# Matmul columns taken in pieces by turns from two halves, and operands set apart, in an fp32r transformer kernel

## What is computed

```python
h = h + 0.5 * swiglu(rms_norm(h, ffn1_norm), ffn1_wi, ffn1_wo)   # halves a1, b1, c1
h = h + mixer(rms_norm(h, mix_norm))                             # gla, dsa, mla
h = h + 0.5 * swiglu(rms_norm(h, ffn2_norm), ffn2_wi, ffn2_wo)   # halves a2, b2, c2
def swiglu(x, wi, wo):
    gate, up = jnp.split(x @ wi, 2, axis=-1)                     # 1024 -> 2 * 2816
    return (jax.nn.silu(gate) * up) @ wo                         # 2816 -> 1024
```

## Time and profile before

| | |
|---|---|
| median of 2 runs | 1460.05 us (1460.01 to 1460.09) |
| the profiled execution | 1459.98 us |
| its span, first to last instruction | 1458.1 us |
| TensorE busy | 1451.5 us, granted clock 1.0 of 2.4 GHz |
| weight loads busy | 1250.3 us |
| VectorE busy | 1002.2 us (69%) |
| ScalarE busy | 777.7 us (53%) |
| DMA | 183 GB/s mean |

### The profile page before, as it was taken

How to read it: one execution, slowest core, us unless ns; L and a number is a source line. 1 busy time by engine, 2 the same in 40 slices (tenths; PEclk the granted TensorE clock), 3 DMA queues, 4 the chain that set the end, 5 groups by cost and what they waited for, 6 DMA issues and landing times.

```text
span 1458.1 us, 18627 instructions
## 1 busy us (share of the span) xinstructions
PE 1451.5 (100%) x7822; PEld 1250.3 (86%) x7822; DVE 1002.2 (69%) x1216; ACT 777.7 (53%) x971; POOL 87.1 (6%) x113
## 2 busy tenths in 40 slices
PE   9999999999999999999999999999999999999999
PEld 7888888888888888888888888888888888888887
DVE  6876466777755877459877764787646987687753
ACT  6654355655534555345665544565436876465542
POOL 0000003000000000006100000000000800000000
PEclk9999999999999999999999999999999999999999
DMA  9855563556556555545465556465556543566552
GB/s 328 277 176 185 159 204 116 167 180 201 178 184 200 190 181 195 185 141 172 149 200 188 185 177 206 154 223 182 188 173 217 188 145 118 173 196 201 179 188 72
DMA packets 205620, 266.82 MB, mean 183 GB/s; under 512 B 6944, under 2 KB 148880, under 8 KB 205280
## 3 DMA queue, kind: packets, MB, share of 16 engines
q1 hardware_dynamic: 204320, 261.23, 54.7%
q0 software_dynamic: 1072, 4.35, 0.8%
q10 hardware_dynamic: 144, 0.05, 0.0%
HBM read 264.56 MB, written 1.05 MB: 182 GB/s over the span
## 4 chain that ended last, share of the span: by engine, by line
PE 93%; DVE 3%; ACT 1%; DMA 1%; issue 0%; SPq 0%; DVEq 0%; ACTq 0%
PE ps L631 31%; PE ps L638 17%; PE ps L563 14%; PE ps L565 13%; PE ps L564 13%; PE ps L616 1%; DMA raw<-in_ffn_wi 1%; DVE wlo L1656 1%; PE ps L741 1%; PE ps L836 1%; PE ps L774 1%; DVE d_i L2049 0%; ACT whi L1217 0%; DVE d_m L2045 0%; DVE d_i L2073 0%
## 5 line engine op out<-in xcount | busy, mean ns | idle before, releaser
L1656 DVE TENSOR_TENSOR wlo<-raw,whi 128x2048 fp32r<-128x2048 f32 (+5 forms) x275 | 567.3, 2068 | 259.1 <-ACT whi L1217 258.9
L1217 ACT CAST whi<-raw 128x2048 fp32r<-128x2048 f32 (+5 forms) x275 | 474.0, 1729 | 223.0 <-PE ps L565 218.5
L631 PE MATMUL ps<-xt,whi 128*128 128x512 f32 x2112 | 501.7, 391 | 0.8 <-DVE xt L2249 0.7
L631 PEld LDWEIGHTS ps<-xt,whi 128*128 128x128 f32 x2112 | 389.3, 188 | 78.0 <-DVE xt L2249 1.5
L638 PEld LDWEIGHTS ps<-xt,wlo 128*128 128x128 f32 x2112 | 267.1, 191 | 8.2
L638 PE MATMUL ps<-xt,wlo 128*128 128x256 f32 x2112 | 269.6, 283 | 0.0
L563 PE MATMUL ps<-whi,xt 128*128 128x512 f32 (+4 forms) x304 | 112.7, 371 | 0.0
L565 PE MATMUL ps<-whi,xt 128*128 128x512 f32 (+4 forms) x304 | 109.7, 361 | 0.0
L564 PE MATMUL ps<-wlo,xt 128*128 128x512 f32 (+4 forms) x304 | 109.5, 360 | 0.0
L563 PEld LDWEIGHTS ps<-whi,xt 128*128 128x128 f32 x304 | 57.3, 189 | 9.2 <-issue 1.0
L565 PEld LDWEIGHTS ps<-whi,xt 128*128 128x128 f32 x304 | 57.2, 188 | 8.5
(11 more groups left out here) (422 smaller groups left out, 1884.3 us busy)
## 6 DMA issues: line engine op xcount, KB each, us to landing
raw<-in_ffn_wi SPq DMA_DIRECT2D x85, 1024.0 KB, 5.0
raw<-in_ffn_wo SPq DMA_DIRECT2D x40, 1024.0 KB, 4.9
raw<-in_ffn_w_gate SPq DMA_DIRECT2D x22, 1024.0 KB, 5.1
raw<-in_ffn_w_up SPq DMA_DIRECT2D x22, 1024.0 KB, 5.1
raw<-in_ffn_w_down SPq DMA_DIRECT2D x20, 1024.0 KB, 4.9
raw<-in_w_in SPq DMA_DIRECT2D x14, 1024.0 KB, 5.1
raw<-in_even_w_in SPq DMA_DIRECT2D x6, 1024.0 KB, 5.2
raw<-in_ffn_wo SPq DMA_DIRECT2D x8, 512.0 KB, 3.8
```

What stands on the lines that cost most here:

```text
L631: return e.matmul(Pair(job.name).ap[:, b, :], whi[:, v % SPLIT, 256 * j + 128 * b:256 * j + 128 * b + 128], XS[:, j, :, :].rearrange("p h ...
L1217: e.copy(whi[0:n, v % SPLIT, c], raw[0:n, v % RAW, c]).then_inc(s_hi.mark(*[(v, j) for j in js]), 1)
L1656: e.tensor_tensor(wlo[0:n, v % SPLIT, c], raw[0:n, v % RAW, c], whi[0:n, v % SPLIT, c].bitcast(F32), ALU.subtract).then_inc(s_lo.mark(*[(v ...
```

## The change

A new function `in_step` reorders the columns of a matmul. It cuts the moving operand into two halves, and takes a piece from the first, a piece from the second, the next piece from the first, and so on. The output access is reordered in the same way, so each column lands where it did and the sums are the same. A table `PIECE` gives the length of a piece for each half in elements of 4 bytes, and 16 holds everywhere else. Widths that don't divide by two pieces stay as they were.

A second table, `PLACE`, moves the activations by 0, 16, 32 or 48 elements inside buffers that are a little larger. `xt` gets another start for each stage, `ht` is one buffer for both parts, and so is `yt`.

```diff
+PLACE = {"in": 0, "gla": 16, "a2": 48, "dsa": 32, "b2": 32, "mla": 32}
+PIECE = {"in": 16, "gla": 16, "a2": 16, "dsa": 8, "b2": 32, "mla": 128}
+
+
+def in_step(ap, piece=16):
+
+    n = ap.shape[1]
+    if n % (2 * piece):
+        return ap
+    return ap.rearrange("p (h g i) -> p g h i", h=2, i=piece)
+
+
...
     def room(self, sb):
-        self.hT = Turned(sb(self.name + "ht_hi", [128, 22, 256], F32R), sb(self.name + "ht_lo", [128, 22, 256], F32R))
+        at = (PLACE[self.x] + 32) % 64
+        room = sb(self.name + "ht", [128, 2 * 22 * 256 + 64], F32R)[:, at:at + 11264].rearrange("p (h k t) -> p h k t", h=2, k=22)
+        self.hT = Turned(room[:, 0], room[:, 1])
...
+        xs_room = sb("xt", [128, 4096 + 64], F32R)
+
+        def x_turned(x):
+            at = PLACE.get(x, 32)
+            XS = xs_room[:, at:at + 4096].rearrange("p (k h t) -> p k h t", k=8, h=2)
...
+        yt_room = sb("yt", [128, 4096 + 32], F32R)[:, 32:].rearrange("p (h k t) -> p h k t", h=2, k=8)
+        YT = Turned(yt_room[:, 0], yt_room[:, 1])
...
-                    o = pair.ap[:, tt, 0:wd]
+                    piece = next((f.piece for f in (a1, a2, b1, b2, c1, c2) if job in f.d), 16)
+                    o, hi_w, lo_w = (in_step(a, piece) for a in (pair.ap[:, tt, 0:wd], hi_w, lo_w))
...
-                    return e.matmul(Pair(job.name).ap[:, b, :], whi[:, v % SPLIT, 256 * j + 128 * b:256 * j + 128 * b + 128],
-                                    XS[:, j, :, :].rearrange("p h t -> p (h t)"), start=j == 0, stop=stop)
+                    return e.matmul(in_step(Pair(job.name).ap[:, b, :], f.piece), whi[:, v % SPLIT, 256 * j + 128 * b:256 * j + 128 * b + 128],
+                                    f.XS[:, j, :, :].rearrange("p h (g i) -> p g h i", i=f.piece), start=j == 0, stop=stop)
...
-                    return e.matmul(Pair(job.name).ap[:, b, 0:256], wlo[:, v % SPLIT, 256 * j + 128 * b:256 * j + 128 * b + 128],
-                                    XS[:, j, 0, :], start=False, stop=stop)
+                    return e.matmul(in_step(Pair(job.name).ap[:, b, 0:256], f.piece), wlo[:, v % SPLIT, 256 * j + 128 * b:256 * j + 128 * b + 128],
+                                    in_step(f.XS[:, j, 0, :], f.piece), start=False, stop=stop)
```

More of the change, by code:

```diff
@@ L156, in __init__ @@
     def __init__(self, name, x, gate, g0, up, u0, down, XT):
-        self.name, self.x = name, x
-        self.g = [Job(f"{name}g{i}", gate, [(0, 8, 128)], [(g0 + 256 * i, 256)], XT, ("xt", x)) for i in range(11)]
-        self.u = [Job(f"{name}u{i}", up, [(0, 8, 128)], [(u0 + 256 * i, 256)], XT, ("xt", x)) for i in range(11)]
+        self.name, self.x, self.XS, self.piece = name, x, XT[x].XS, PIECE[x]
+        self.g = [Job(f"{name}g{i}", gate, [(0, 8, 128)], [(g0 + 256 * i, 256)], XT[x], ("xt", x)) for i in range(11)]
+        self.u = [Job(f"{name}u{i}", up, [(0, 8, 128)], [(u0 + 256 * i, 256)], XT[x], ("xt", x)) for i in range(11)]
         self.d = [Job(f"{name}d{i}", down, full_blocks(FF), [(512 * i, 512)], None, (name, "ht")) for i in range(2)]
@@ L230, in program @@
         XR = X[:, :, :].rearrange("p t d -> p (t d)").rearrange("p (k t) -> p k t", k=8)
-        XS = sb("xt", [128, 8, 2, 256], F32R)
-        XT = Turned(XS[:, :, 0, :], XS[:, :, 1, :])
-        YT = Turned(sb("yt_hi", [128, 8, 256], F32R), sb("yt_lo", [128, 8, 256], F32R))
+        xs_room = sb("xt", [128, 4096 + 64], F32R)
+        def x_turned(x):
+            at = PLACE.get(x, 32)
+            XS = xs_room[:, at:at + 4096].rearrange("p (k h t) -> p k h t", k=8, h=2)
+            t = Turned(XS[:, :, 0, :], XS[:, :, 1, :])
+            t.XS = XS
+            return t
+        XT = {x: x_turned(x) for x in ("in", "a1", "gla", "a2", "b1", "dsa", "b2", "c1", "mixed", "mla")}
+        yt_room = sb("yt", [128, 4096 + 32], F32R)[:, 32:].rearrange("p (h k t) -> p h k t", h=2, k=8)
+        YT = Turned(yt_room[:, 0], yt_room[:, 1])
         G = sb("G", [128, 128])
@@ L572, in last_steps @@
                 for tt, c0, n in ((0, 0, wd), (1, 0, wd // 2), (1, wd // 2, wd // 2)):
-                    o = own.ap[:, c0 // (wd // 2), 0:n] if tt else pair.ap[:, 0, :]
+                    o = in_step(own.ap[:, c0 // (wd // 2), 0:n] if tt else pair.ap[:, 0, :])
                     for j in range(nk):
@@ L577, in last_steps @@
                         q.wait_ge(*s_lo[v, j])
-                        hi_w, lo_w = (w[:, v % SPLIT, j * wd + c0:j * wd + c0 + n] for w in (whi, wlo))
+                        hi_w, lo_w = (in_step(w[:, v % SPLIT, j * wd + c0:j * wd + c0 + n]) for w in (whi, wlo))
                         h, l = (a[:, kt, 128 * tt:128 * tt + 128] for a in (job.act.hi, job.act.lo))
@@ L1595, in mla @@
                 unit()
[L1596 removed]
+                turned(("mixt", 0), XT["mixed"], 0, None)
                 unit()
                 unit()
[L1599 removed]
+                turned(("mixt", 1), XT["mixed"], 4, None)
                 unit()
@@ L1613, in x_high @@
                 q.wait_ge(*s_xt[min(j // 2, 2)]["x"])
-                e.mul(XT.hi[:, j, :], XR[:, j, :], gain("f1", j)).then_inc(s_act.mark(("x0", j)), 1)
+                e.mul(XT["in"].hi[:, j, :], XR[:, j, :], gain("f1", j)).then_inc(s_act.mark(("x0", j)), 1)
             x_high(0)
@@ L2248, in x_low @@
                 q.wait_ge(*s_act["x0", j])
-                e.scalar_tensor_tensor(XT.lo[:, j, :], XR[:, j, :], gain("f1", j), XT.hi[:, j, :].bitcast(F32),
+                e.scalar_tensor_tensor(XT["in"].lo[:, j, :], XR[:, j, :], gain("f1", j), XT["in"].hi[:, j, :].bitcast(F32),
                                        ALU.mult, ALU.subtract).then_inc(s_dve.mark((("xt", "in"), j)), 1)
```

20 lines of the change are left out of this document (10 added, 10 removed).

## The result

The changed kernel takes 1514.07 us (median of 2 runs, 1513.99 to 1514.14) and the one before 1460.05. That is a ratio of 1.037, with a 95% interval from 1.0354 to 1.0387: slower by 54 us, where 1413 us was predicted. The page of the changed kernel has these lines, which answer to the earlier trace rows. The columns of a group are line, engine, operation, forms, count, then busy us and mean ns of one.

What follows compares the result with a forecast made beforehand. TensorE was taken to bound the kernel. Gains of 10.1 (b2), 7.6 (c1), 15.1 (a2, b1), 2.5 (a1) and 11.9 (mixers) summed to 47.2 us, giving 1413 us against 1460; the range was 1381 to 1478.

Steps and rivals of the forecast that it cites:

- TensorE bounds the kernel: Whole kernel: TensorE is busy 1451.5 of 1458.1 us, so time is the number of matmuls times the distance between starts.
- 13.3 ns extra at 512 and at 256 columns: Each matmul step: 226.7 ns against 213.3 for 512 columns, 119.9 against 106.7 for 256, paid once per matmul.
- Where the 13.3 ns come from: Matmul reads: the moving stream meets the weight load twice, 6.7 ns each; taking halves in turn keeps them in step.
- The 10.4 ns: Gain per matmul where streams stay apart: 13.3 - 2.9 ns, at most 10.07 us for a half's 968 matmuls.
- The plain fp32 rows: dsa's scores: 256 columns at half the column rate take 216.2 ns, only 2.9 extra, so no fixed price.
- The unequal 360-column steps: mla's job: 160 ns in the first slice, 163.8 on average behind it; claimed that the extra depends on addresses.
- The gains per stage: Savings: b2 10.1, c1 7.6, a2 and b1 15.1, a1 2.5, c2 nothing, mixers 11.9 us.
- The control: c2, with pieces of 128: expected to keep steps of 226.7 and 120 ns and gain nothing.
- Turns cost: Rival, chance 0.20: each jump between halves, in read or PSUM write, costs 0 to 0.83 ns; 1531 us at 0.42.
- Nothing changes: Rival, chance 0.15: the extra belongs to fp32r at full rate, 360-column steps differ for their width; 1460 us.
- The distance is wrong: Rival, chance 0.10: 32 is no middle; one or two of a1, a2, b1 gain 10 us each; 1440 to 1450.
- Extra instructions, queues and shifted buffers at nothing: Other engines and DMAs: no instruction added, same DMAs, and shifting buffers by 32 elements hides in ScalarE and VectorE slack.

## Why the prediction was wrong

- **TensorE bounds the kernel.** Right. Its busy time and the span rose together, by 55.3 and 54.2 us, and no other engine's by more than 1.7.
- **13.3 ns extra at 512 and at 256 columns.** The measurement was right; every run of before's layout repeats it.
- **Where the 13.3 ns come from.** This step failed. It read them as two meetings of the moving read with the weight load, which end when both run in step. The load's rate of 1.2 columns per ns, an estimate there, agrees with the rows' durations (188, 136 and 109 ns for 128, 64 and 32 columns). But with the load in step no distance gained, two standing streams 32 apart took 243.4 / 122.2, and with pieces of 16 neither distance nor load length changed anything. The 10.4 ns that the sum takes off per matmul rest on this step, and no stage gained any of it. The sum also has no term for the turns themselves, and the pieces alone cost 50.3 us. The plain fp32 rows don't carry what they were used for: a stream at half the rate having 2.9 ns extra doesn't say that the rest is a meeting. (By the starts of the eight records, 1509 ns for seven steps, that extra is 2.2 ns; the 2.9 carry the rounding of 1.46 us.)
- **The unequal 360-column steps** The earlier trace rows were read rightly as "addresses matter": distance alone moves the steps from 226.7 to as much as 235, and from 120 down to as little as 113.7. What distance brings was read the wrong way. 0 is the best distance for 512 columns, so the change moved five halves and the mixers away from it. The Trainium skill's rule that TensorE's two read ports wait for no one ("SBUF — State Buffer", section "Who interferes with whom") gave 1460 for this. By it the distances alone would do nothing, and they cost 13.7 us; for the turns it has no price.
- **The gains per stage** (10.1, 7.6, 15.1, 2.5, 0 and 11.9 us) were in truth losses: b2 11.1, c1 5.9, a2 and b1 15.7, a1 7.9, c2 2.9 and the mixers 10.8 us. The control failed too: c2 is slower by its distance of 32, not by its pieces.
- **Turns cost** is the rival that came true, at 0.20. The loss of 54.0 us over 169,570 turns is 0.32 ns each, within its bounds of 0 and 0.83, and its sign that b2 is the slowest half held. Its form did not: it took a price per turn, and b2 lost only 1.4 times what a2 did with 2.04 times the turns. It also left read and write together; the write is free. Against it stood "runs of 32 to 128 bytes are long beside one 4-byte column"; what the runs show is that pieces up to 128 bytes cost and pieces of 256 and 512 bytes don't.
- **Nothing changes** fell with the time itself. **The distance is wrong** fell as well: with pieces of 16 the step is 240.0 ns at distances 0, 16 and 48 alike, so none of them gains.
- **Extra instructions, queues and shifted buffers at nothing.** Right, by the windows.

The range up to 1478 left out only this rival. At 0.20 its weight was too low: the Trainium skill's warning and the untested jump were set against a chain of three guesses (rates, map, meeting), each of which had to hold for a gain. The chances have a gap as well: the sum gives 1438 us if only b2 and the mixers gain, yet the mechanism's whole 0.55 lies at 1431 or below.

**What stays open.** What the 13.3 ns at distance 0 are: a shorter or standing load takes 5 to 6 ns from the low step and adds 2 to 5 to those of 512 columns, so the load has a part in it, but nothing tried took a step of 512 below 226.7 or one of 256 below 113.7. Why re-reading 16 columns costs as much as turns. And why a block of low matmuls settles at 113.4 or at 117.8 ns, with the same distance.

## What to carry to other kernels

An access pattern that is "the same bytes in another order" is not free on the moving side: keep the moving fp32r operand in runs of at least 256 bytes that start even with the stationary operand modulo 256 bytes, while the output in PSUM can be taken in pieces of 32 bytes at no cost here. Before building a layout on a mechanism that was read from rates, measure the operation by itself in one stage; here six halves in one kernel gave six settings for one run. If all operands stand at the same place modulo 256 bytes, try activations 64 bytes later for the stages with mixed 512 and 256 column matmuls, and measure it: here it gave 5 us of 1460, while moving the low weights alone cost 7.

## What the runs showed of the hardware

- The price of turns isn't proportional to the columns: with pieces of 16 the step of 256 columns stays at 120.0 (119.6 before), and that of 512 is twice it, 240.0, instead of 226.7.
- Reading columns again that were just read isn't cheaper than a jump: 242.3 ns for 16 columns repeated, 236.6 for 32, 228.2 for 64.
- Where the second half of a 512-column read in pieces of 64 stands 16 or 32 off modulo 64, the step is 233.3 to 236.7 ns, close to the 230 to 235 of one-run reads at distances of 20 to 60.
- A load's row is 188 ns for 128 columns and 196 when they are taken with step 2; the 512-column steps beside the latter are 230.4 to 234.4 ns at six distances.
- One-run matmuls of 256 columns at distances 16 and 48 have two levels, 113.4 and 117.8 ns, and a block of 32 keeps its level from end to end. The same distance of 48 gave 113.4 ns in one kernel and 117.8 in another.
